# Hybrid recurrent decoder step with expert retrieval: later places for the hand-off of finished sub-tiles, and one wait less ahead of a squaring

## The reference

```
for i in range(DEPTH):                       # 2 layers
    h = rmsnorm(x, ln_mix[i])
    o = even_mixer(h, ...) if i % 2 == 0 else odd_mixer(h, ...)
    x = x + o
    x = x + peer_ffn(rmsnorm(x, ln_ffn[i]), ...)
return rmsnorm(x, ln_final), states
```

```
pre = jnp.einsum('thkd,td->thk', u_tab[expert], tb)
act = jax.nn.gelu(pre) * gate
return jnp.einsum('thk,thkd->td', act, v_tab[expert])
```

## Time and profile before

| What | Value |
|---|---|
| median of 3 runs | 3359.38 us (3356.14 to 3359.39) |
| the profiled execution's own time | 3360.97 us |
| its span, first to last instruction | 3359.0 us |
| PE, DVE, ACT, POOL busy | 81%, 63%, 37%, 37% of the span |
| moved by DMA | 1225.88 MB, 365 GB/s over the span |
| indirect gathers of `ring` | 1024 of `picked` rows and 16 of `tail_pick` rows |
| granted TensorE clock, mean | 0.84 |
| first dot product of a unit | at 377.7 us of the span |

### The profile page before, as it was taken

The page is one execution under the profiler, slowest core; times in us unless marked ns, Lnnn a source line. Parts: engine busy times, 40 slices in busy tenths (PEclk is TensorE's granted clock), DMA queues, the critical chain, the costliest instruction groups (busy, mean ns, idle before and its releaser), DMA issues.

```text
span 3359.0 us, 34624 instructions
## 1 busy us (share of the span) xinstructions
PE 2711.8 (81%) x11134; PEld 1371.6 (41%) x11134; DVE 2104.4 (63%) x4889; ACT 1231.8 (37%) x3752; POOL 1241.5 (37%) x1101
## 2 busy tenths in 40 slices
PE   8879997888988689788976789788789666676776
PEld 7767653444544145344522345344344111111132
DVE  4454688775656787576466785566546776744554
ACT  3211365442333343443333343532333343333332
POOL 0100133663433433344343433344333443433442
PEclk9889997996899789799988799797789776766677
DMA  4204698999999999999999999999899999999997
GB/s 158 76 1 176 246 403 329 389 395 375 408 408 395 401 419 395 388 388 387 418 421 421 405 419 409 368 390 413 368 412 372 400 419 421 397 422 422 421 419 327
DMA packets 186152, 1225.88 MB, mean 365 GB/s; under 512 B 21297, under 2 KB 24129, under 8 KB 50802
## 3 DMA queue, kind: packets, MB, share of 16 engines
q0 software_dynamic: 153024, 1115.00, 81.8%
q1 hardware_dynamic: 32946, 108.67, 8.6%
HBM read 1211.74 MB, written 11.84 MB: 364 GB/s over the span
## 4 chain that ended last, share of the span: by engine, by line
PE 48%; DMA 26%; DVE 15%; ACT 5%; issue 3%; DVEq 2%; POOL 1%; SPq 0%; ACTq 0%; POOLq 0%
PE ps L613 47%; DMA ring<-in_uv,picked 24%; DVE ring L2357 6%; DVEq L2149 1%; ACT scratch L1206 1%; ACT diag L1206 1%; ACT L1206 1%; DVE scratch L2100 1%; ACT gated L1206 1%; DMA scratch<-in_keys 1%; POOL ring L596 1%; ACT act_v L1206 1%; DVE scratch L2118 0%; DVE scratch L2104 0%; DVE ids L2106 0%
## 5 line engine op out<-in xcount | busy, mean ns | idle before, releaser
L596 POOL DMA_INDIRECT ring<-in_uv,picked x1024 | 1166.3, 1139 | 1744.6 <-PE ps L613 1635.3
L613 PE MATMUL ps<-ring,diag 128*64 128x512 f32 x4096 | 1339.8, 749 | 481.6 <-ACT diag L1206 474.7
L2357 DVE SCALAR_TENSOR_TENSOR ring<-ring,htok 128x1024 f32<-128x1024 f32 x1024 | 1243.2, 1227 | 596.0 <-DMA ring<-in_uv,picked 590.8
L613 PE MATMUL ps<-hT,wring 128*128 128x256 f32 (+1 forms) x3200 | 802.1, 401 | 18.4 <-DVE hT L1600 8.7
L1206 ACT ACTIVATE act_v<-pre 128x1 f32<-128x1 f32 x1040 | 209.5, 201 | 1467.3 <-DVE ring L2357 1466.3
L613 PEld LDWEIGHTS ps<-hT,wring 128*128 128x128 f32 x3200 | 602.6, 195 | 326.2 <-issue 229.8
L613 PEld LDWEIGHTS ps<-ring,diag 128*64 128x64 f32 x4096 | 245.1, 156 | 1188.4 <-ACT diag L1206 997.6
L1206 ACT ACTIVATE diag<-folded,gated 128x64 f32<-128x64 f32 x1024 | 356.2, 348 | 36.0 <-PE ps L613 2.7
L1206 ACT ACTIVATE gated<-act_v,gates 128x1 f32<-128x1 f32 x1024 | 301.7, 295 | 33.3
L613 PEld LDWEIGHTS ps<-scratch 128*128 128x128 f32 (+2 forms) x1428 | 201.5, 209 | 147.6 <-issue 85.5
L613 PE MATMUL ps<-scratch 128*128 128x128 f32 (+5 forms) x1428 | 238.0, 312 | 28.4 <-DVE scratch L1747 15.1
(11 more groups left out here) (340 smaller groups left out, 1734.3 us busy)
## 6 DMA issues: line engine op xcount, KB each, us to landing
wring<-in_weights SPq DMA_DIRECT2D x200, 512.0 KB, 7.8
ring<-in_uv,picked POOLq DMA_INDIRECT x1024, 13.3
scratch<-in_keys POOLq DMA_DIRECT2D x4, 1024.0 KB, 14.6
scratch<-in_s_gla POOLq DMA_DIRECT2D x4, 1024.0 KB, 12.7
out_o_gla<-scratch POOLq DMA_DIRECT2D x4, 1024.0 KB, 12.8
scratch<-in_s_dn POOLq DMA_DIRECT2D x1, 2048.0 KB, 14.4
scratch<-in_s_ssm POOLq DMA_DIRECT2D x1, 2048.0 KB, 19.9
out_o_dn<-scratch POOLq DMA_DIRECT2D x1, 2048.0 KB, 11.8
```

The source lines that it names most:

```text
L596: pool.indirect_dma_start(out=ring[:, g % RING, :], out_offset=None, in_=io["uv"][L], in_offset=bass.IndirectOffsetOnAxis(ap=index, axis=0 ...
L613: return pe.matmul(out, lhsT, rhs, start=start, stop=stop)
L2357: stt(x, x, 1.0, h, MUL, MUL, accum_out=pre[:, g % SMALL:g % SMALL + 1]).then_inc(sem("dotted"), 1)
```

## The change

The one set of places (2, 4, 4, 6) becomes two: `SOON` with these numbers for sub-tiles 3, 7, 11 and 15, and `LATE` with copy at 3, turn at 7, add at 14, fold from 17 for all others. The turn and the add now have different places. The waits on the two state stores ahead of the squaring go.

```
-COPY_AT, TURN_AT, FOLD_AT = 2, 4, 6
+LATE, SOON = (3, 7, 14, 17), (2, 4, 4, 6)
+
+
+def handoff(w):
+    return SOON if w % 4 == 3 else LATE
...
 def rows_off(u):
     off = part_off(u, 3) + 2 if u in BESIDE else 5
-    return max(off, FIRST[ROW_TILE[u] - 1] + FOLD_AT + 7 - TOPK_AT[u][0])
+    return max(off, fold_slot(2 * ROW_TILE[u] - 1) + 7 - TOPK_AT[u][0])
 
 
 def fold_slot(w):
-    at = SUB_FIRST[w - 1] + FOLD_AT
+    at = SUB_FIRST[w - 1] + handoff(w - 2)[3]
...
-        FINAL = ((0, 256, 12, 784), (256, 192, 15, SUB_FIRST[15] + TURN_AT + 2))
+        FINAL = ((0, 256, 12, 784), (256, 192, 15, SUB_FIRST[15] + handoff(14)[2] + 2))
...
-                    if g == SUB_FIRST[w] + TURN_AT and w:
+                    if w and g == SUB_FIRST[w] + handoff(w - 1)[1]:
                         turn(w - 1)
...
                 act.wait_ge(sem("mixed"), 3 + p)
-                if p:
-                    act.wait_ge(sem("gla_chunk_stored0"), 32)
-                    act.wait_ge(sem("gla_chunk_stored1"), 32)
                 f(o_sq[:, :, 0:n], hT[:, :, 0:n], ACT.Square).then_inc(sem("sq_ready"), 1)
...
-                    if g == SUB_FIRST[w] + COPY_AT and w:
+                    if w and g == SUB_FIRST[w] + handoff(w - 1)[0]:
                         copy_out(w - 1)
...
-                    if g == SUB_FIRST[w] + TURN_AT and w:
+                    if w and g == SUB_FIRST[w] + handoff(w - 1)[2]:
                         add_out(w - 1)
```

## The result

| | before | after |
|---|---|---|
| median of the timed runs | 3357.76 us (4 runs, 3353.45 to 3359.39) | 3337.66 us (4 runs, 3335.47 to 3340.27) |
| profiled execution, span | 3360.97 us, 3359.0 us | 3337.3 us, 3335.4 us |
| busy PE, DVE, ACT, POOL | 2711.8, 2104.4, 1231.8, 1241.5 us | 2698.5, 2112.6, 1233.0, 1243.7 us |

The ratio is 0.9935, 95% interval 0.9922 to 0.9947: 20.1 us less between the medians. The forecast was 17.9 less (3341.5) in a range from 3325 to 3353.

A forecast was written before the change was run, and what follows sets the result against it. No one engine bounds the whole; DMA is full in two long stages. Hand-offs 9.7 plus waits 7.8 make 17.5 us off the profiled 3360.97, so 3343.5, about 3341.5 as a median; range 3325 to 3353.

The forecast's parts named there:

- the two waits: Slot 678: without the state-store waits ACT squares 7.77 us earlier; the second pair, ahead of the query copies, gives 0.
- sub-tiles 3 and 11: PE's idle 2.23 us behind turn and tile goes at each; net 2.2 each, 4.4 together.
- sub-tiles 5 and 9: PE's idle 1.00 us and a fold half of 1.03 leave each; some comes back later; net 1.0 each.
- The wait's total: DVE's addition waited 96.4 us for PE's turn, 15 times; this sum was said not to be the gain.
- The four hand-offs in full DMA: Sub-tiles 6, 7, 14 and 15: removing DVE's waits is worth 0, because DMA is full.
- What is late next is ACT itself: Slot 678 after the waits go: ACT arrives only with unit 678, so PE still waits some 6 us.
- Sub-tile 1: DVE's next scan step starts 3.45 us earlier; part is given back later in the scan; net 1.3 us.
- The charge of 2.17: Sub-tile 1's give-back later in the scan: addition 0.69, turn 0.45, first fold half 1.03 us.
- Sub-tile 2: DVE's 3.97 us from turn to delta step go, but folds and addition land where PE is busy; net -0.6.
- The 4.53 charged: Sub-tile 2's cost behind slot 144: two fold halves of 1.92 us at clock 0.53, 3.84, and the addition.
- Sub-tiles 10 and 13: Sub-tile 10: PE's idle 2.56 us, capped by DMA, gives 1.0; sub-tile 13: DVE's 1.58 us wait gives 1.6.
- The clock rival: Less idle time also raises PE's clock in three stretches, 12.9 us more, giving 3328.6 us; chance 0.15.

The follow-up runs named there:

- the first experiments: Kernel before profiled again unchanged, 3361.75 us; then, each on the kernel before, only the two state-store waits removed, ratio 0.9974, and only the later places, ratio 0.9966.
- the nearer place: Changed kernel with the late places cut to copy 2, turn 4, addition 8, fold 10: ratio 0.9915 of the kernel before.
- full DMA only: Changed kernel with late places only in sub-tiles 6, 7, 14 and 15, old ones elsewhere, state-store waits dropped: ratio 0.9984 of the kernel before.
- before once more: The kernel before, unchanged, profiled a second time: 3361.75 us.
- waits only: Kernel before without the two state-store waits, all hand-off places as before: ratio 0.9974 of the kernel before.

## Why the prediction was right, and where its terms were not

The time (3337.7 against 3341.5), the sign and the range held. The mechanism did too for the two waits, for sub-tiles 1 and 2 and for sub-tiles 3 and 11, where the late starts and the idle times went as forecast, and the sums of the two halves are 8.7 and 11.4 us against 7.8 and 9.7. At sub-tiles 5 and 9 it did not: the idle time there stayed.

- *The wait's total is not the gain.* 96.4 us of waits went, 11.4 us of time came. The four hand-offs in full DMA brought nothing that can be measured, as forecast.
- *The two waits.* 7.8 forecast from 7.77, 8.6 by the stage (5.46 instead of 13.74 us of PE's idle time is 8.28). "What is late next is ACT itself" and PE "near 6" held. POOL's gap is 8.47, not near 12. Counted from the start of PE's gap (the start of its sums less the number in the bracket), POOL's last gather ended 1.24 us later in before and 3.35 in after, and PE's sums, behind which POOL goes on, are shorter too.
- *Sub-tile 1.* Mis-sized: 1.3 forecast, 4.1 measured. The 3.45 gross was right. The charge of 2.17 for addition, turn and fold half did not show in the stage. How much is paid goes with the place: with the same work at 4, 8 and 10 the gain is 1.6 of the 4.1.
- *Sub-tile 2.* The 3.97 gross came (3.9 in every late trace). The 4.53 charged was too much: the stage from 140 to 150 is no longer with the folds in it than without, by the medians. The step that failed is "a half of the fold takes 1.92 us at that clock". It took the clock as given, while behind the fold it was higher in five traces of six (after's first half took 1.50 us, its second 1.02). Of the whole 6.8 us in after's own trace, only about 2.4 belong to the change.
- *Sub-tiles 3 and 11.* 2.2 each forecast. Sub-tile 11 gave 2.1. Sub-tile 3 gave 4.4 by medians that hold 1.0 to 5.7 us of waits for the keys. Less these waits the two gave 2.6 and 1.6, 4.2 together against 4.4.
- *Sub-tiles 5 and 9.* 1.0 each forecast. Sub-tile 9 gave 1.3, within the scatter. Sub-tile 5 failed. The step that failed is "PE idles 1.00 us in each, behind a fold half of 1.03 that leaves this place: 2.03". The idle time did not leave with the fold half: in units 320 to 346 it was 17.5 to 18.6 us and became 19.7 to 20.6. What came there were 2.6 us at a higher clock, and then 4.3 were lost at a lower one in units 346 to 384, where I had charged 1.03 for the moved pieces.
- *Sub-tiles 10 and 13.* 1.0 and 1.6 forecast, 1.6 and 1.0 measured; sub-tile 10's idle time fell by 1.5 of the 2.56 us.
- *The clock rival* (3328.6) did not come. Of its three places the clock rose at one, units 320 to 346, and fell right behind it. In units 648 to 676 it is 0.74 to 0.77 in all traces, and in units 676 to 690 it is 0.69 to 0.71 with the two waits and 0.68 to 0.80 without. The mean over the span is 0.840 and 0.836 in the two traces of before and 0.844 in after; before's timed runs beside the first experiments have 0.839 to 0.846, after's 0.840 to 0.846, so no change shows.

By the stage medians about 25 us came where 17.5 were forecast: 8.0 too little at sub-tiles 1, 2 and 3, and 2.8 too much at 5 and at 6 and 7, are the large errors. That the timed runs came within 2.2 us of the forecast owes something to these two signs, and to the scatter of single stages.

## What to carry to other kernels

A wait that has a total of 96 us on an engine is worth only what starts late behind it on the engine or queue that is short at that place. Read it wait by wait, with the idle time of the next engine and the DMA share beside it. When a hand-off is moved, a few units of distance are enough: four did what seven did, and in sub-tile 5 the nearer place kept a gain that the farther one lost again. A shorter stage is not yet a shorter wait: look whether the idle time went or the clock rose, for the clock fell again here. A load whose landing time scatters should be issued with that scatter as its margin, as the keys show: three units earlier were worth 2.1 and 5.8 us by the two stages, against -0.9 to 4.4 of a stage with moved hand-offs.

## What was not expected of the hardware

- The same load of 1 MB, in a stretch where DMA was at 0.97 to 1.02 of its time, landed from 12.46 to 16.98 us after its issue (13.76 in before, 12.48 with full DMA only, and by the end of PE's wait 13.71 in before once more and 15.73 with waits only). PE's wait for it went from 1.01 to 5.67 us with it.
- PE was busy for 20 of 20 us with the clock at 0.53, while it worked groups of one-column products. With a fold half of four products of 512 columns among them the next group ran in 1.95 to 2.02 instead of 3.57 us in five traces of six, and not in the sixth.
- In sub-tile 5, units 346 to 384 took 2.7 to 4.4 us longer in the five traces with late places than in the median of the six with old ones, at a lower clock (0.76 against 0.83 in the windows shown), though the idle time ahead of the slow products was the same 2.37 us. With the nearer places they took 1.2 and 1.5 us longer, at the clock of the old ones. The cause stays open.
